# A hybrid decoder step on one core: sample attention taken four batches at a time, with zero-padded queries and probabilities

## The chip, the cores and the metric

The kernel runs on one core of one Trainium2 chip. The metric is the device time of one launch in microseconds (us). Three unprofiled runs of the kernel before took 1790.85, 1792.77 and 1795.26 us, so its median is 1792.77 us. One profiled execution, whose rows are quoted below, took 1795.69 us.

## The reference

One layer of a decoder with two parallel groups of heads is computed for 256 prompt tokens and for 8 sample batches of 8 new tokens each (320 token columns in all), model width 2048:

```python
p = rmsnorm(x) @ w_in                       # 3*1024 attention columns, 4*1024 delta-rule columns, 16 more
att = attend(q_att, k_att, v_att)           # 8 heads of 128
gdn = gated_delta_rule(...)                 # 8 heads of 128
x = x + concat(att, gdn) @ w_out
x = x + conv_ffn(rmsnorm(x))                # 2048 -> 2*5632 -> 2048
```

The part that is changed is `attend` for the sample tokens. Each of the 8 batches has 256 past keys and values in two pages of 128 rows of a paged cache, named by a page table, and its own 8 new tokens:

```python
lo = einsum('bqhd,bkhd->bqhk', q, k_own) * scale + rel_bias(own)    # causal inside the batch
ls = einsum('bqhd,bqhsd->bqhs', q, k_past) * scale + rel_bias(past)
p  = softmax(concat([ls, lo]))
out = p[..., :256] @ v_past + p[..., 256:] @ v_own
```

## The kernel before

**The stream of projections.** All weight products run on TensorE as a stream of chunks. A chunk is 512 rows by 256 columns of a weight: it is loaded by a queue of SyncE, split by ScalarE (`w_hi`, L687) and VectorE (`w_lo`, L1044) into a high and a low part, three chunks ahead of its use, and used in 24 matmuls with 320 moving columns (lines L1554 to L1556). There are 144 chunks before the feed-forward part (`g0`, `g1`, `a0`, `a1`, `wg`, `wa0`, `wa1`: the input projection by groups of heads, then the output projection) and 264 in it.

**Small steps between the quarters.** The delta rule and the attention are cut into steps such as `("P", "SS", g, b)`: the engine (P TensorE, A ScalarE, V VectorE, G GpSimd), the name, the half `g` of the heads (4 heads each) and a batch. `schedule()` places the chain of steps into the quarters of the chunks. A quarter is 6 projection matmuls and counts 10 units; a TensorE step adds 0.85 times its entry in `LENGTH` to the clock `at`; a step of another engine pushes back `ready`, the earliest place of the next TensorE step, by its `LENGTH` less 1 (GpSimd: less 4); no step is placed before the chunk that stands beside it in the chain. Each engine then works through its own list in this order, and waits by semaphores for the steps that it needs. Nothing of the schedule is known to the chip: where a step comes too early, TensorE waits and the projections wait behind it. GpSimd has nothing between its steps here, so it issues a load as soon as its semaphores allow.

**Attention steps of the half g** (`att_steps`): `hk` loads and flips the table of relative biases (hankel, 512 KB) and VectorE writes `bias_q` and `bias_s` from it; `kv` turns the new keys and values and stores them; `S`, `E`, `N`, `T`, `O` are the prompt's attention head by head. Then, for each batch b of the sample tokens:

- `pk`, `pv`: GpSimd reads two page numbers and issues two loads of 256 KB each, of keys and of values, two batches deep in `k_pages` and `v_pages`.
- `kt`: 8 transposes of key pages on TensorE; ScalarE and VectorE copy one half each to `k_t_past` (L861, L1347).
- `SS`: scores; for each head one matmul of 8 query columns against 256 past keys (L1907) and one against the 64 new keys (L1908), the four heads at the partitions 0, 32, 64 and 96 of the output.
- `SS`, `SE`, `SN` on VectorE, ScalarE, VectorE: scale, bias and maximum (L1352 to L1356); exponential and sum (L864); reciprocal and product (L1359, L1360).
- `PT`: three transposes of the probabilities, copied by ScalarE; `PV`: 8 matmuls on the pages (L1921) and 4 on the new values (L1924), each with 8 columns of probabilities stationary; `OT`: one transpose back.

The planner puts `SS` of one batch next to `OT` of the batch before it. In its slots, the first half's `hk` on TensorE stands in chunk 88 (quarter 3), `kv` in 92 (1), the first `kt` in 98 (0) and the last `OT` in 110 (3). The second half starts in chunk 113, its first `kt` stands in 119 (3) and its last `OT` in 132 (2). The output projection's last part begins at chunk 136 and needs them.

Of the kernel before, what the change touches and what calls it, by code (L numbers as in the profile page):

```python
# [17 lines left out]
F32 = mybir.dt.float32  # L18
# [6 lines left out]
P = 128  # L25
# [23 lines left out]
def constants():  # L49
# [15 lines left out]
    }  # L65
    cb, rb = np.arange(BLK)[None, :], r % BLK
# [178 lines left out]


def ffn_param_steps():
    s = []
    for r in range(5):
# [144 lines left out]
def build(nc, I, O):  # L394
# [80 lines left out]
    kst = a.put("k_tok", [P, 2, 4, P])  # L475
    hk = a.put("hankel", [P, 4, 2 * P])
    bm = a.put("bias_q", [P, 4, 2 * P])
    bs = a.put("bias_s", [P, 2 * P + 120])
    sc = a.put("scores", [P, 2, 384])
    pt = a.put("probs_t", [P, 2, 384])  # L480
    ktp = a.put("k_t_past", [P, 4, 2 * P])
    kp = a.put("k_pages", [P, 2, 2, 4, P])
    vp = a.put("v_pages", [P, 2, 2, 4, P])
# [45 lines left out]

    def over_free(ap, count):  # L530

        return ap.unsqueeze(2).broadcast_to([ap.shape[0], ap.shape[1], count])
# [18 lines left out]
    def sem(name):  # L551
        sems[name] = nc.alloc_semaphore(name)
        return sems[name]
# [12 lines left out]
    pk_in, pv_in, s_in, s_out = ([sem(f"{k}{i}") for i in range(2)] for k in ("k_pages_in", "v_pages_in", "state_in", "state_out"))  # L566
# [53 lines left out]
    with block:  # L620
# [57 lines left out]
        def _(act):  # L678
# [51 lines left out]
            def step(x):  # L730
# [131 lines left out]
                elif name == "SE":  # L862
                    after(act, "V", "SS", *k)
                    finish(act.activation(sc[:, 0, 0:TOK], sc[:, 0, 0:TOK], ACT.Exp, bias=ast[:, 0, 0:1], accum_out=ast[:, 0, 2:3]))  # L864
                elif name == "PT":
                    after(act, "P", "PT", *k)
                    act.activation(pt[:, 0, 0:256], b3[:, 0:256], ACT.Copy)
                    finish(act.activation(pt[0:NS, 0, 256:384], b3[0:NS, 256:384], ACT.Copy))
                elif name == "PV":
                    after(act, "P", "PV", *k)  # L870
                    finish(act.activation(ob[:, :], b0[:, 0:P], ACT.Copy))
                elif name == "OT":
                    g, b = k
                    after(act, "P", "OT", *k)
                    finish(act.activation(reg[g][:, 0:4, SEQ + b * DT:SEQ + b * DT + DT],
                                          b1[:, 0:P].rearrange("p (h s) -> p h s", h=4)[:, :, 0:DT], ACT.Copy))
# [6 lines left out]
                elif name == "ma":  # L883
                    g = k[0]
                    act.wait_ge(mm_done, FIRST["wg"])
                    after(act, "A", "OT", g, DB - 1)
# [144 lines left out]
        def _(dve):  # L1031
# [59 lines left out]
            def step(x):  # L1091
# [218 lines left out]
                elif name == "hk":  # L1310
                    g = k[0]
                    after(dve, "P", "hk", g)
                    chain(dve.tensor_copy(bm[:, :, :], psB[:, 2:4, :].rearrange("p k (h x) -> p (k h) x", h=2)))
                    if g == 0:
                        dve.memset(bs[:, 0:2 * P], 0.0)
                        dve.memset(bs[:, 2 * P:], NEG)
                    chain(tt(bm[:, :, P:2 * P], bm[:, :, P:2 * P], over_heads(C("causal"), 4), ALU.add))
                    for h in range(4):
                        row = bs[32 * h:32 * h + DT]
                        dve.tensor_copy(row[:, 0:P], bm[0:DT, h, 0:1].broadcast_to([DT, P]))  # L1320
                        dve.tensor_copy(row[:, P:2 * P], bm[0:DT, h, 0:P])
                        ins = dve.tensor_copy(row[:, 2 * P + 56:2 * P + 64], bm[0:DT, h, P:P + DT])
                    finish(ins)
# [21 lines left out]
                elif name == "kt":  # L1345
                    after(dve, "P", "kt", *k)
                    finish(dve.tensor_copy(ktp[:, :, P:2 * P], heads(b1, P)))  # L1347
                elif name == "SS":
                    g, b = k
                    after(dve, "P", "SS", g, b)  # L1350
                    o_ = 2 * P + 56 - DT * b
                    dve.scalar_tensor_tensor(out=sc[:, 0, 0:256], in0=b2[:, 0:256], scalar=SCALE, in1=bs[:, 0:256],  # L1352
                                             op0=ALU.mult, op1=ALU.add)
                    chain(dve.scalar_tensor_tensor(out=sc[:, 0, 256:TOK], in0=b2[:, 256:TOK], scalar=SCALE,
                                                   in1=bs[:, o_:o_ + NS], op0=ALU.mult, op1=ALU.add))
                    finish(dve.tensor_reduce(ast[:, 0, 0:1], sc[:, 0, 0:TOK], AX.X, ALU.max, negate=True))  # L1356
                elif name == "SN":
                    after(dve, "A", "SE", *k)
                    chain(dve.reciprocal(ast[:, 0, 4:5], ast[:, 0, 2:3]))  # L1359
                    finish(dve.tensor_scalar(sc[:, 0, 0:TOK], sc[:, 0, 0:TOK], ast[:, 0, 4:5], None, ALU.mult))  # L1360
# [181 lines left out]
        def _(pe):  # L1542
# [54 lines left out]
            def step(x):  # L1597
# [251 lines left out]
                elif name == "hk":  # L1849
                    g = k[0]  # L1850
                    pe.wait_ge(hk_in, 16 * (g + 1))
                    after(pe, *(("V", "us", 1, 3) if g == 0 else ("A", "OT", 0, DB - 1)))
# [4 lines left out]
                elif name == "kv":  # L1857
# [3 lines left out]
                    after(pe, *(("A", "kv", g, t - 1) if t else ("V", "hk", g)))  # L1861
# [21 lines left out]
                elif name == "O":  # L1883
# [5 lines left out]
                    finish(pe.matmul(b3[:, P:SEQ], vt[:, 1, h, :], pt[:, h % 2, SEQ:SEQ + P], start=False, stop=True))  # L1889
                elif name == "kt":  # L1890
                    g, b = k
                    pe.wait_ge(pk_in[b % 2], 32 * (DB // 2 * g + b // 2 + 1))
                    after(pe, *(("A", "O", g, 3) if b == 0 else ("V", "SS", g, b - 1)))
                    if b >= 2:
                        after(pe, "A", "OT", g, b - 2)
# [4 lines left out]
                elif name == "SS":  # L1900
                    g, b = k
                    after(pe, "A", "kt", g, b)
                    after(pe, "V", "kt", g, b)
                    c0 = SEQ + b * DT
# [381 lines left out]
```

## Time and profile before

| | |
|---|---|
| median of three runs | 1792.77 us (1790.85 to 1795.26) |
| the profiled execution | 1795.69 us, of which the span from first to last instruction is 1794.0 us |
| TensorE busy | 1700.9 us, 95% of the span |
| VectorE, ScalarE, GpSimd busy | 1070.7, 665.4, 206.0 us |
| mean granted TensorE clock | 0.989 |
| bytes moved by DMA | 258.29 MB, 144 GB/s in the mean |

Busy time says how long an engine had work in it, not how fast it got on; the place where this kernel's time is set is read from the starts of the projection matmuls, which follow each other evenly wherever nothing comes between them.

### The profile page before, as it was taken

Reading aid. Unit: us, or ns where it says so; the run is one execution under the profiler, and the core shown is the slowest. Engines: PE = TensorE matmul, PEld = TensorE weight load, DVE = VectorE, ACT = ScalarE, POOL = GpSimd, SP = SyncE. Lnnn points to the kernel's source line nnn. Section 1 sums busy time; section 2 is a strip of 40 time slices with the busy share of each in tenths; the row PEclk is TensorE's granted clock in tenths of the full one; section 3 lists DMA queues with packets and bytes.
Section 4 is the critical chain, followed back from the end, with each engine's and each line's share of the span. In section 5 each row is a group of like instructions: output and inputs, shape, how many; then the busy total and the mean of one; then the engine's idle time right before and its main releaser. Section 6 shows DMA issues by size and latency. Waiting matters only on the chain.

```text
span 1794.0 us, 31685 instructions
## 1 busy us (share of the span) xinstructions
PE 1700.9 (95%) x13245; PEld 1618.7 (90%) x13245; DVE 1070.7 (60%) x1744; ACT 665.4 (37%) x932; POOL 206.0 (11%) x343
## 2 busy tenths in 40 slices
PE   4999998899988988999999999999999999999996
PEld 3998987898778778789999999999999999999995
DVE  5456676665534444456676666666667565666662
ACT  4453432443224444445333333333333333333332
POOL 1112123112121110100010000000000000000010
PEclk9999999999999999999999999999999999999999
DMA  6333345433574553533444444444444444444432
GB/s 184 108 117 108 106 124 155 128 106 113 165 235 134 185 186 123 189 121 122 147 150 155 149 146 152 142 157 149 153 153 147 148 153 153 144 150 153 152 128 68
DMA packets 229998, 258.29 MB, mean 144 GB/s; under 512 B 9052, under 2 KB 220574, under 8 KB 229216
## 3 DMA queue, kind: packets, MB, share of 16 engines
q1 hardware_dynamic: 216448, 220.14, 38.5%
q0 software_dynamic: 10720, 34.86, 6.4%
q8 instruction: 105, 1.72, 0.4%
q10 hardware_dynamic: 2688, 1.27, 0.3%
q14 instruction: 37, 0.30, 0.1%
HBM read 245.11 MB, written 11.12 MB: 143 GB/s over the span
## 4 chain that ended last, share of the span: by engine, by line
PE 79%; DVE 10%; issue 4%; DMA 3%; ACT 3%; POOL 1%; DVEq 0%; SPq 0%; POOLq 0%; ACTq 0%
PE ps_proj L1554 18%; PE ps_proj L1556 18%; PE ps_proj L1555 18%; PE ps_small L1554 5%; PE ps_small L1556 5%; PE ps_small L1555 5%; DVE w_lo L1044 3%; PE ps_small L1589 2%; ACT w_hi L687 2%; DMA state_s<-in_state_gdn_dram 1%; DMA x_raw<-in_x_sample_dram 1%; DVE conv_acc L1065 1%; DVE state_s L1039 1%; DMA out_ss_dram<-state_s 1%; PE ps_small L1921 0%
## 5 line engine op out<-in xcount | busy, mean ns | idle before, releaser
L1554 PE MATMUL ps_proj<-x_hi,w_hi 128*128 128x320 f32 x2560 | 822.7, 321 | 8.8 <-DVE x_lo L1039 4.6
L1556 PE MATMUL ps_proj<-x_hi,w_lo 128*128 128x320 f32 x2560 | 795.3, 311 | 0.0
L1555 PE MATMUL ps_proj<-x_lo,w_hi 128*128 128x320 f32 x2560 | 795.2, 311 | 0.0
L1044 DVE TENSOR_TENSOR w_lo<-w_raw,w_hi 128x1024 fp32r<-128x1024 f32 x408 | 506.2, 1242 | 456.1 <-ACT w_hi L687 455.0
L687 ACT ACTIVATE w_hi<-w_raw 128x1024 fp32r<-128x1024 f32 x408 | 431.3, 1058 | 719.5 <-PE ps_proj L1556 524.2
L1554 PEld LDWEIGHTS ps_proj<-x_hi,w_hi 128*128 128x128 f32 x2560 | 485.2, 190 | 30.5 <-issue 18.5
L1555 PEld LDWEIGHTS ps_proj<-x_lo,w_hi 128*128 128x128 f32 x2560 | 485.7, 190 | 2.4 <-issue 1.7
L1556 PEld LDWEIGHTS ps_proj<-x_hi,w_lo 128*128 128x128 f32 x2560 | 484.7, 189 | 0.0
L1554 PE MATMUL ps_small<-hid_hi,w_hi 128*128 128x320 f32 x704 | 218.2, 310 | 0.0
L1556 PE MATMUL ps_small<-hid_hi,w_lo 128*128 128x320 f32 x704 | 217.5, 309 | 0.0
L1555 PE MATMUL ps_small<-hid_lo,w_hi 128*128 128x320 f32 x704 | 217.5, 309 | 0.0
L2229 POOL TENSOR_TENSOR ffn_ext<-ffn_params_t,consts 128x16 f32<-128x16 f32 x88 | 52.4, 617 | 839.2 <-DVE ffn_acc L1437 814.8
L1554 PEld LDWEIGHTS ps_small<-hid_hi,w_hi 128*128 128x128 f32 x704 | 132.2, 188 | 1.6 <-DVE x_res L1039 1.6
L1555 PEld LDWEIGHTS ps_small<-hid_lo,w_hi 128*128 128x128 f32 x704 | 132.2, 188 | 0.0
L1556 PEld LDWEIGHTS ps_small<-hid_hi,w_lo 128*128 128x128 f32 x704 | 132.2, 188 | 0.0
L1039 DVE TENSOR_TENSOR x_res<-ps_small,x_res 128x640 f32<-128x640 f32 x88 | 72.4, 823 | 60.6 <-PE ps_small L1556 60.6
L1437 DVE SCALAR_TENSOR_TENSOR ffn_acc<-ffn_ext,ffn_params_t,ffn_acc 128x336 f32<-128x336 f32 x176 | 94.3, 567 | 3.9
L1039 DVE TENSOR_TENSOR ffn_ext<-ps_proj,root 128x512 f32<-128x512 f32 x132 | 41.7, 373 | 0.0
L1065 DVE SCALAR_TENSOR_TENSOR conv_acc<-u_ext,params_t,conv_acc 128x344 f32<-128x344 f32 x72 | 38.2, 572 | 0.6
L1435 DVE TENSOR_SCALAR ffn_acc<-ffn_ext,ffn_params_t 128x336 f32<-128x336 f32 x88 | 36.9, 451 | 0.0
L2073 POOL TENSOR_TENSOR small<-small 128x4 f32<-128x4 f32 (+5 forms) x17 | 22.0, 1297 | 105.3 <-DVE small L1279 31.4
L958 ACT ACTIVATE ffn_acc<-ffn_acc 128x672 f32<-128x672 f32 x22 | 16.9, 769 | 38.8 <-DVE ffn_acc L1437 38.8
(326 smaller groups left out, 1190.5 us busy)
## 6 DMA issues: line engine op xcount, KB each, us to landing
w_raw<-in_w_up_dram SPq DMA_DIRECT2D x176, 512.0 KB, 3.5
w_raw<-in_w_in_dram SPq DMA_DIRECT2D x112, 512.0 KB, 3.5
w_raw<-in_w_down_dram SPq DMA_DIRECT2D x88, 512.0 KB, 3.3
w_raw<-in_w_out_dram SPq DMA_DIRECT2D x32, 512.0 KB, 3.3
state_s<-in_state_gdn_dram POOLq DMA_DIRECT2D x16, 512.0 KB, 5.6
k_pages<-in_cache_k_dram POOLq DMA_DIRECT2D x32, 256.0 KB, 3.6
v_pages<-in_cache_v_dram POOLq DMA_DIRECT2D x32, 256.0 KB, 3.4
out_ss_dram<-state_s POOLq DMA_DIRECT2D x8, 512.0 KB, 4.5
```

The costliest lines, as they stand in the source:

```text
L687: act.activation(whi[:, slot], raw[:, slot], ACT.Copy).then_inc(hi_done, 1)
L1039: return dve.tensor_tensor(out, a_, b_, op)
L1044: dve.tensor_tensor(wlo[:, slot], raw[:, slot], whi[:, slot].bitcast(F32), ALU.subtract).then_inc(lo_done, 1)
L1065: ins = dve.scalar_tensor_tensor(out=acc[:, j, 0:344], in0=u, scalar=wcol, in1=acc[:, j, 0:344], op0=ALU.mult, op1=ALU.add)
L1435: ins = dve.tensor_scalar(facc[:, kind, j, 0:336], u, w_(2), w_(3), ALU.mult, ALU.add)
L1437: ins = dve.scalar_tensor_tensor(out=facc[:, kind, j, 0:336], in0=u, scalar=w_(tap), in1=facc[:, kind, j, 0:336], op0=ALU.mult, op1=ALU.add)
L1554: pe.matmul(o, hi, rhs_hi[:, k0 + kk_, :], start=first and kk_ == 0, stop=False)
L1555: pe.matmul(o, hi, rhs_lo[:, k0 + kk_, :], start=False, stop=False)
L1556: ins = pe.matmul(o, lo, rhs_hi[:, k0 + kk_, :], start=False, stop=last and kk_ == CQ - 1)
L1589: return pe.transpose(out, in_, C("ident", n, n))
L2073: return pool.tensor_tensor(out, in_, sm("mh", n, 0, width), ALU.pow)
L2229: ins = pool.tensor_tensor(fue[:, kind, j, 2 + SEQ:338].rearrange("p (b s) -> p b s", b=DB)[:, :, 0:2], old, C("ones", P, 16).rearrange("p ...
```

## The change

For the sample tokens, four batches share one softmax. The 32 queries of four batches and one head fill 32 partitions. `q_z` holds them as four blocks that are zero but for the 8 queries of one batch, so the scores of four batches add up in one PSUM tile: `SS` still runs per batch, with 32 stationary columns, and the product with the new keys runs once per four. The steps `SS`, `SE`, `SN` of VectorE and ScalarE, and `PT`, `PV`, `OT`, run twice per half instead of eight times. ScalarE copies the transposed probabilities into zeroed blocks (`probs_z`), so that `PV` adds up four batches. GpSimd clears both (`qz`), VectorE fills the queries. `bias_s` is made by a new pair of steps `hb`: four matmuls that repeat the first 8 rows over 32 partitions, and five VectorE instructions in place of twelve small copies. `v_pages` grows to four batches, the biases' table shares its space with the fourth, so the second table is loaded after the first half's last `PV` instead of right behind the first `hk`. `k_pages` stays at two. In the order, `kt` of the next batch follows `SS` at once, and `PT`, `PV`, `OT` of the first four batches are spread over the batches 4 to 6. `LENGTH` gets new values.

```diff
+    parts["rep8"] = r == np.arange(32)[None, :] % DT
+    parts["own"] = own
+    parts["ownneg"] = np.where(own, 0.0, NEG)
...
 def att_steps(g):
-    s = ([] if g else [("G", "hk", g)]) + [("G", "pk", g, 0), ("G", "pv", g, 0), ("G", "pk", g, 1), ("G", "pv", g, 1), ("P", "hk", g), ("V", "hk", g)]
-    if g == 0:
-        s += [("G", "hk", 1)]
+    s = [("G", "hk", g), ("G", "pk", g, 0)] + [("G", "pv", g, b) for b in range(3)] + [("G", "pk", g, 1), ("P", "hk", g), ("V", "hk", g)]
+    s += [("G", "pv", g, 3), ("P", "hb", g), ("V", "hb", g)]
...
-    s += [("P", "kt", g, 0), ("A", "kt", g, 0), ("V", "kt", g, 0), ("G", "pk", g, 2)]
-    for b in range(DB):
-        s += [("P", "SS", g, b), ("V", "SS", g, b), ("A", "SE", g, b)]
-        if b < DB - 1:
-            s += [("P", "kt", g, b + 1), ("A", "kt", g, b + 1), ("V", "kt", g, b + 1)]
-            if b < DB - 3:
-                s += [("G", "pk", g, b + 3)]
-        s += [("V", "SN", g, b), ("P", "PT", g, b), ("A", "PT", g, b), ("P", "PV", g, b),
-              ("A", "PV", g, b), ("P", "OT", g, b), ("A", "OT", g, b)]
-        if b < DB - 2:
-            s += [("G", "pv", g, b + 2)]
+    s += [("P", "kt", g, 0), ("G", "qz", g), ("A", "kt", g, 0), ("V", "kt", g, 0), ("V", "qz", g, 0)]
+    soft = []
+    for q in range(2):
+        for b in range(4 * q, 4 * q + 4):
+            s += [("P", "SS", g, b)]
+            if b < DB - 2:
+                s += [("G", "pk", g, b + 2)]
+            s += soft[:1]
+            if b < DB - 1:
+                s += [("P", "kt", g, b + 1)] + soft[1:3] + [("A", "kt", g, b + 1), ("V", "kt", g, b + 1)]
+            soft = soft[3:]
+            if b == 3:
+                s += [("V", "SS", g, 0), ("V", "qz", g, 1), ("A", "SE", g, 0), ("V", "SN", g, 0)]
+                soft = [("P", "PT", g, 0), ("A", "PT", g, 0), None,
+                        ("P", "PV", g, 0), ("A", "PV", g, 0), None,
+                        ("P", "OT", g, 0), ("A", "OT", g, 0), None]
+            s = [x for x in s if x]
+            if ("P", "PV", g, 0) in s and ("G", "pv", g, 4) not in s:
+                s += [("G", "pv", g, 4 + j) for j in range(4)]
+    s += [("V", "SS", g, 1), ("A", "SE", g, 1), ("V", "SN", g, 1), ("P", "PT", g, 1), ("A", "PT", g, 1), ("P", "PV", g, 1),
+          ("A", "PV", g, 1), ("P", "OT", g, 1), ("A", "OT", g, 1)]
...
-          "ks": 13, "us": 22, "sh": 11, "hk": 20, "kv": 12, "S": 11, "O": 12, "kt": 17, "SS": 11, "PV": 11, "OT": 2, "ab": 76},
-    "A": {"sc2": 25, "sc5": 20, "ab": 10, "qs": 12, "cp": 0, "tb1": 10, "o": 12, "kv": 12, "E": 11, "SE": 7, "fp": 22},
+          "ks": 13, "us": 22, "sh": 11, "hk": 20, "kv": 12, "S": 11, "O": 12, "kt": 10, "hb": 6, "SS": 6, "PT": 4, "PV": 16, "OT": 2, "ab": 76},
+    "A": {"sc2": 25, "sc5": 20, "ab": 10, "qs": 12, "cp": 0, "tb1": 10, "o": 12, "kv": 12, "E": 11, "SE": 9, "kt": 8, "PT": 9, "fp": 22},
...
-          "S": 13, "SS": 17, "SN": 7},
-    "G": {"rn": 29, "or": 14, "so": 0, "si": 0, "s2": 0, "gs": 0, "kv": 0, "pk": 0, "pv": 0, "hk": 100, "mk": 6, "xd": 0},
+          "S": 13, "SS": 15, "SN": 7, "kt": 8, "hb": 12, "qz": 3},
+    "G": {"rn": 29, "or": 14, "so": 0, "si": 0, "s2": 0, "gs": 0, "kv": 0, "pk": 0, "pv": 0, "hk": 100, "mk": 6, "xd": 0, "qz": 0},
...
+                    for h in range(4):
+                        ins = pe.matmul(b2[32 * h:32 * h + 32, 0:P + DT], C("rep8"), bm[:, h, 0:P + DT], start=True, stop=True)
...
-                    for h in range(4):
-                        qT = reg[g][:, h, c0:c0 + DT]
-                        pe.matmul(b2[32 * h:32 * h + DT, 0:256], qT, ktp[:, h, :], start=True, stop=True)
-                        ins = pe.matmul(b2[32 * h:32 * h + DT, 256:TOK], qT, reg[g][:, 4 + h, SEQ:TOK], start=True, stop=True)
+                    if j == 0:
+                        after(pe, "V", "qz", g, q)
+                        if q:
+                            after(pe, "V", "SS", g, 0)
+                        for h in range(4):
+                            pe.matmul(b2[32 * h:32 * h + 32, 256:TOK], reg[g][:, h, SEQ + 32 * q:SEQ + 32 * q + 32],
+                                      reg[g][:, 4 + h, SEQ:TOK], start=True, stop=True)
+                    for h in range(4):
+                        ins = pe.matmul(b2[32 * h:32 * h + 32, 0:256], qz[:, P * j + 32 * h:P * j + 32 * h + 32], ktp[:, h, :],
+                                        start=j == 0, stop=j == 3, skip_group_check=True)
...
+                    for j in range(4):
+                        pe.wait_ge(pv_in[j], 32 * (2 * g + q + 1))
+                        for i in range(2):
+                            for h in range(4):
+                                at = P * j + 32 * h
+                                pe.matmul(b3[32 * h:32 * h + 32, 384:512], pz[:, i, at:at + 32], vp[:, j, i, h, :],
+                                          start=j == 0 and i == 0, stop=False, skip_group_check=True)
...
-                        after(pool, "P", "hk", 0)
+                        after(pool, "P", "PV", 0, 1)
...
+                elif name == "qz":
+                    g = k[0]
+                    after(pool, "A", "O", g, 3)
+                    for i in range(2):
+                        pool.wait_ge(kv_out[i], 32 * ((2, 1), (3, 3))[g][i])
+                    pool.memset(qz[:, :], 0.0)
+                    finish(pool.memset(pz[:, :, :], 0.0))
```

`probs_z` is 2 by 544 columns and `q_z` 544; ScalarE's `PT` copies become two of 128 by 128 into the blocks of `probs_z` and one of 64 by 128.

## Rows read from the trace of the kernel before

**Rows 1.** The page: busy time, share of the span and instructions of each engine

```profile
PE 1700.9 (95%) x13245; PEld 1618.7 (90%) x13245; DVE 1070.7 (60%) x1744; ACT 665.4 (37%) x932; POOL 206.0 (11%) x343
```

**Rows 2.** TensorE's waits, 520 to 860 us: total, times, longest

```profile
PE ps_small L1589 <- DVE scores L1360: 8.8, 12, 1.4
...
PE ps_small L1589 <- DVE bias_s L1322: 1.5, 1, 1.5
...
PE ps_small L1907 <- DVE k_t_past L1347: 0.7, 1, 0.7
```

**Rows 3.** Timeline of TensorE around one batch: start, us, instruction, idle time before

```profile
575.68 0.39 PE L1554 MATMUL ps_proj<-x_hi,w_hi 128*128 128x320 f32 x1
...
577.74 0.55 PE L1589 MATMUL ps_small<-consts,scores 128*128 128x128 f32 x3 [0.94 <-DVE scores L1360]
578.04 0.39 PE L1554 MATMUL ps_proj<-x_hi,w_hi 128*128 128x320 f32 x1
...
579.09 0.62 PE L1921 MATMUL ps_small<-v_pages,probs_t 128*8 128x128 f32 x16
579.64 0.40 PE L1924 MATMUL ps_small<-v_tok,probs_t 64*8 64x128 f32 x8
579.98 0.42 PE L1554 MATMUL ps_proj<-x_hi,w_hi 128*128 128x320 f32 x1
...
581.16 0.64 PE L1907 MATMUL ps_small<-k_t_past,reg 128*8 128x256 f32 x8
581.59 0.32 PE L1908 MATMUL ps_small<-reg 128*8 128x64 f32 x8
581.84 0.41 PE L1554 MATMUL ps_proj<-x_hi,w_hi 128*128 128x320 f32 x1
582.09 0.31 PE L1555 MATMUL ps_proj<-x_lo,w_hi 128*128 128x320 f32 x1
...
584.28 0.31 PE L1555 MATMUL ps_proj<-x_lo,w_hi 128*128 128x320 f32 x1
...
585.37 0.39 PE L1554 MATMUL ps_proj<-x_hi,w_hi 128*128 128x320 f32 x1
```

**Rows 4.** Timeline of TensorE: a step of the delta rule with 32 stationary columns

```profile
468.44 1.08 PE L1827 MATMUL ps_small<-state_s,reg 128*32 128x128 f32 x32 [0.40 <-DMA state_s<-in_state_gdn_dram]
```

**Rows 5.** Groups of VectorE and of ScalarE, 569 to 650 us, shapes apart

```profile
L1044 DVE TENSOR_TENSOR w_lo<-w_raw,w_hi 128x1024 fp32r<-128x1024 f32 x14 | 17.2, 1225 | 26.9 <-ACT w_hi L687 26.9
...
L861 ACT ACTIVATE k_t_past<-ps_small 128x512 f32<-128x512 f32 x8 | 4.8, 599 | 4.9 <-PE ps_small L1589 4.9
```

**Rows 6.** Timeline of GpSimd: the two key pages of batch 3 as they are issued

```profile
577.13 0.67 POOL L2182 DMA_DIRECT2D k_pages<-in_cache_k_dram  x1 [4.02 <-issue]
578.27 0.55 POOL L2182 DMA_DIRECT2D k_pages<-in_cache_k_dram  x1 [0.47 <-issue]
```

**Rows 7.** The page: DMA issues, KB each, us from issue to landing

```profile
state_s<-in_state_gdn_dram POOLq DMA_DIRECT2D x16, 512.0 KB, 5.6
k_pages<-in_cache_k_dram POOLq DMA_DIRECT2D x32, 256.0 KB, 3.6
v_pages<-in_cache_v_dram POOLq DMA_DIRECT2D x32, 256.0 KB, 3.4
```

**Rows 8.** Timeline of TensorE: the first bias table

```profile
517.69 3.78 PE L1854 MATMUL ps_small<-hankel,consts 128*128 128x512 f32 x4 [7.11 <-DMA hankel<-rb_scratch]
```

**Rows 9.** Groups of GpSimd: clearing 1024 columns

```profile
L2111 POOL MEMSET reg<- 128x1024 f32 x2 | 1.9, 975 | 0.0
```

**Rows 10.** Stretches: PE, PEld, DVE, ACT, POOL busy, clock, DMA share, GB/s

```profile
516.00:522.00 6.00, 4.31 (x7) 2.24 (x8) 0.49 (x1) 0.00 (x0) 2.58 (x5) 0.50 0.74 251
652.00:658.60 6.60, 5.99 (x22) 6.02 (x23) 3.05 (x3) 1.68 (x3) 0.00 (x0) 0.50 0.26 86
696.30:699.60 3.30, 3.30 (x15) 3.30 (x14) 0.22 (x1) 2.42 (x6) 0.00 (x0) 0.50 0.00 0
569.00:650.00 81.00, 75.59 (x746) 64.99 (x744) 34.24 (x62) 33.31 (x74) 17.58 (x32) 1.00 0.58 189
```

More of the change, by code:

```diff
@@ L474, in build @@
     vt = a.put("v_tok", [P, 3, 4, P])
[L475 to L478, printed above, removed]
+    kst_at = a.at
+    pz = a.put("probs_z", [P, 2, 4 * (P + DT)])
+    kst = nc.alloc_sbuf_tensor_at("k_tok", [P, 2, 4, P], F32, offset=kst_at)
+    po = a.put("probs_own", [P, P])
+    ktp_at = a.at
+    ktp = a.put("k_t_past", [P, 4, 2 * P])
+    bm = nc.alloc_sbuf_tensor_at("bias_q", [P, 4, 2 * P], F32, offset=ktp_at)
+    bs = a.put("bias_s", [P, 2 * P + 96])
     sc = a.put("scores", [P, 2, 384])
+    pt_at = a.at
     pt = a.put("probs_t", [P, 2, 384])
-    ktp = a.put("k_t_past", [P, 4, 2 * P])
+    qz = nc.alloc_sbuf_tensor_at("q_z", [P, 4 * (P + DT)], F32, offset=pt_at)
     kp = a.put("k_pages", [P, 2, 2, 4, P])
-    vp = a.put("v_pages", [P, 2, 2, 4, P])
+    vp_at = a.at
+    vp = a.put("v_pages", [P, 4, 2, 4, P])
+    hk = nc.alloc_sbuf_tensor_at("hankel", [P, 4, 2 * P], F32, offset=vp_at + 3 * 4096)
     ob = a.put("o_tok", [P, P])
@@ L1313, in step @@
                     chain(dve.tensor_copy(bm[:, :, :], psB[:, 2:4, :].rearrange("p k (h x) -> p (k h) x", h=2)))
+                    finish(tt(bm[:, :, P:2 * P], bm[:, :, P:2 * P], over_heads(C("causal"), 4), ALU.add))
+                elif name == "hb":
+                    g = k[0]
+                    after(dve, "P", "hb", g)
                     if g == 0:
-                        dve.memset(bs[:, 0:2 * P], 0.0)
-                        dve.memset(bs[:, 2 * P:], NEG)
-                    chain(tt(bm[:, :, P:2 * P], bm[:, :, P:2 * P], over_heads(C("causal"), 4), ALU.add))
-                    for h in range(4):
[L1319 to L1323, printed above, removed]
+                        dve.memset(bs[:, 2 * P:2 * P + 32], NEG)
+                        dve.memset(bs[:, 2 * P + 64:], NEG)
+                    dve.tensor_copy(bs[:, 0:P], b2[:, 0:1].broadcast_to([P, P]))
+                    dve.tensor_copy(bs[:, P:2 * P], b2[:, 0:P])
+                    win = bs[:, 2 * P + 32:2 * P + 64].rearrange("p (j s) -> p j s", j=4)
+                    chain(tt(win, over_heads(b2[:, P:P + DT], 4), over_free(C("own"), DT), ALU.mult))
+                    finish(tt(win, win, over_free(C("ownneg"), DT), ALU.add))
                 elif name == "S":
@@ L1889, in step @@
                     finish(pe.matmul(b3[:, P:SEQ], vt[:, 1, h, :], pt[:, h % 2, SEQ:SEQ + P], start=False, stop=True))
+                elif name == "hb":
+                    g = k[0]
+                    after(pe, "V", "hk", g)
+                    for h in range(4):
+                        ins = pe.matmul(b2[32 * h:32 * h + 32, 0:P + DT], C("rep8"), bm[:, h, 0:P + DT], start=True, stop=True)
+                    finish(ins)
                 elif name == "kt":
@@ L1909, in step @@
                     finish(ins)
                 elif name == "PT":
+                    q = k[1]
                     after(pe, "V", "SN", *k)
-                    turn(b3[:, 0:P], sc[:, 0, 0:P], P)
-                    turn(b3[:, P:2 * P], sc[:, 0, P:2 * P], P)
-                    finish(turn(b3[0:NS, 2 * P:3 * P], sc[:, 0, 2 * P:TOK], P))
+                    after(pe, *(("A", "OT", k[0], 0) if q else ("A", "O", k[0], 3)))
+                    turn(b3[:, 0:P], sc[:, q, 0:P], P)
+                    turn(b3[:, P:2 * P], sc[:, q, P:2 * P], P)
@@ L1915, in step @@
+                    finish(turn(b3[0:NS, 2 * P:3 * P], sc[:, q, 2 * P:TOK], P))
                 elif name == "PV":
-                    g, b = k
-                    pe.wait_ge(pv_in[b % 2], 32 * (DB // 2 * g + b // 2 + 1))
-                    after(pe, "A", "PT", g, b)
-                    for i in range(2):
-                        for h in range(4):
-                            pe.matmul(b0[32 * h:32 * h + DT, 0:P], pt[:, 0, i * P + 32 * h:i * P + 32 * h + DT],
-                                      vp[:, b % 2, i, h, :], start=i == 0, stop=False)
+                    g, q = k
@@ L1923, in step @@
                     for h in range(4):
[L1924 to L1925 removed]
+                        ins = pe.matmul(b3[32 * h:32 * h + 32, 384:512], po[0:NS, 32 * h:32 * h + 32], vt[0:NS, 2, h, :],
+                                        start=False, stop=True, skip_group_check=True)
                     finish(ins)
@@ L1928, in step @@
                     after(pe, "A", "PV", *k)
-                    finish(turn(b1[:, 0:P], ob[:, :], P))
+                    finish(turn(b3[:, 0:P], ob[:, :], P))
                 elif name == "fp":
@@ L2172, in step @@
                     g, b = k
+                    if name == "pk":
+                        slot = b % 2
+                        if b > 1 or g:
+                            after(pool, "P", "kt", *((g, b - 2) if b > 1 else (0, DB - 2 + b)))
+                        cache, tile_, arrived = I["cache_k"], kp, pk_in
+                    else:
+                        slot = b % 4
+                        if b > 3 or g:
+                            after(pool, "P", "PV", *((g, 0) if b > 3 else (0, 1)))
+                        if b == 3:
+                            after(pool, "P", "hk", g)
+                        cache, tile_, arrived = I["cache_v"], vp, pv_in
                     if (g, b) == (0, 0):
```

75 lines of the change are left out of this document (45 added, 30 removed).

## The prediction

> **What bounds the kernel.** I read the page first: TensorE has work for 1700.9 of 1794.0 us, VectorE for 60% [rows 1]. So time is worth having only on TensorE's queue, in two kinds: work taken out of it, and waits taken out of it. Next the list of TensorE's waits over the attention [rows 2]: no wait on weights is in it, but 12 waits on the sample tokens' softmax, 8.8 us, and single ones of 0.7 and 1.5 us. Last the timeline of one batch [rows 3], the main source. The projections start every 2.19 / 15 = 0.146 us (582.09 to 584.28). Whatever stretches an interval between two projections beyond 0.146 us for each, a small step has put into the queue.
>
> **Price of a batch before** [rows 3], each interval less its projections:
> - `PT`, 575.68 to 578.04, 6 projections (0.88): 1.48 us. Of it 0.94 is the wait. Three transposes are three eighths of `kt`'s price, 0.34; the remaining 0.20 is the restart after a wait.
> - `PV`, to 579.98: 1.06.
> - `OT` and `SS`, to 581.84: 0.98; `OT` is one transpose, 0.11, so `SS` is 0.87.
> - `kt`, to 585.37, 18 projections: 0.90.
>
> Work without waits: 0.34 + 1.06 + 0.98 + 0.90 = 3.28 us, times 16 batches = 52.5 us. Waits: 8.8 + 12 x 0.2 = 11.2, and 0.7 and 1.5: 13.4 us [rows 2].
>
> **The same work after.** `kt` stays, 16 x 0.90 = 14.4. In `SS` the four heads' passes run side by side: from 581.16 to 581.59 two sets of 256 columns pass in 0.43, so 64 columns cost 0.054 a set. Two such sets leave twelve of the sixteen batches: `SS` is 0.76 x 16 = 12.2, and 0.4 for the four that remain. `PT` and `OT` run four times: 1.4 and 0.4. `PV` had 24 passes in 6 sets of four, and now has 18 sets. A set of 128 columns takes 0.11 us with 32 stationary columns (32 passes in 1.08, the last one's own 0.27 taken off [rows 4]) and (0.62 - 0.27) / 3 = 0.12 with 8 [rows 3]: padding to 32 columns is free. So `PV` is 1.06 + 12 x 0.11 = 2.38, times 4 = 9.5. The new `hb` is an `SS` with 136 in place of 256 columns, 0.56, twice: 1.1. Sum 39.4 us: **13.1 us less work**. The bounds: if `SS` and `kt`, now adjacent, save one restart, 16 x 0.1 less; if 32 columns paid twice for a set, 8 more for `PV`.
>
> The Trainium skill, "TensorE: Matmul & The Clock Gate", section "LDWEIGHTS (loading the stationary operand)", speaks against the padding: the load takes as long as its columns, at 1.2 GHz. Four loads of 32 columns would then need 107 ns a set and hold back only the sets of 64 columns; by that rule the sum would lose an estimated 0.4 us. The trace has no such set at 32 columns.
>
> **Where the steps go.** By the planner's arithmetic `hk` of the first half comes one quarter earlier, since one more GpSimd step of -4 units stands before it (88, quarter 2). `kv` no longer waits for the second table's 96 units: 90 (2), and the first `kt` 96 (1). In the batches a `kt` and the next `SS` are two quarters apart; the lap is 2 x 0.88 + 0.76 + 0.90 = 3.4 us, where before it was 585.37 - 575.68 = 9.7. The last `OT` stands in 102 (1). The second half begins in 113 as before, its `hk` 9 quarters later, its first `kt` in 122 (2), its end in 128 (2), eight chunks before `wa1`. So no deadline is touched, but **the cover of every wait shrinks to a third**. The waits after:
>
> - *Key pages.* GpSimd may load batch b+2 once `kt` of b is done. The second page of batch 3 is issued at 578.27 [rows 6] and takes 3.6 us [rows 7]: there at 581.9, 6.2 us after TensorE left `kt` at 575.68. The new order wants it after 3.4 + 1.75 + 0.76 = 5.9. So 0.3 us is missing twice in each half (batches 2 and 4; the odd ones gain what the even ones lost, and behind batch 4 five quarters of softmax follow). If landings take 5.6, the longest of GpSimd's page-sized loads [rows 7], 2.3 is missing. I take 1.0, nearer to the row of pages: 4 x 1.0 = 4.0.
> - *Copies of `kt` before `SS`.* Two quarters are 1.75 us. The copy takes 0.60 on ScalarE; VectorE may first finish a weight part of 1.23 [rows 5]: about 0.5 missing when it does, for about a third of 14: 14 x 0.15 = 2.1 (nothing to 7). `SS` of batch 6 stands one quarter behind its `kt`; that case costs 0.7 in the trace [rows 2] when the weight part is in the way: 2 x 0.5.
> - *Softmax.* The first four's has more than a batch of cover. The last four's has three quarters, 2.6 us. In the trace the lap from `SS` to its probabilities is longer than the 4 quarters and a `kt` it was given, by 0.94 [rows 3], weight part and `kt` copy included. I take 1.0 twice (nothing to 2.3: both weight parts).
> - *Value pages for the last four.* They are issued together, some 9 us for eight issues 1.14 apart [rows 6], and land 3.4 later, about 12.9 after the first `PV`. The second `PV` reaches its fourth batch after about as long; 0.5 for the load on the DMA engines, 0.3 for the third copy of `PT`, twice: 1.6 (nothing to 5).
> - *`hb` before `kv`:* 0.3 twice. *First bias table:* TensorE already waits 7.1 us for it [rows 8]; a quarter earlier means 0.9 more, since the load comes no sooner. The second table is loaded some ten chunks ahead and hides.
> - *Clearing on GpSimd:* 1632 columns at 0.975 us a thousand [rows 9] are 1.6 us behind the last `O`, and `SS` comes 2.6 behind: hidden, 0.4 to spare once VectorE has filled the queries. It would cost what exceeds that.
>
> Sum 4.0 + 3.1 + 2.0 + 1.6 + 0.6 + 0.9 = 12.2 against 13.4: 1.2 less. ScalarE and VectorE lose work, but they are not the bound. Together 13.1 + 1.2 = **14.3 us less**. The profiled 1795.7 would be 1781.4; it ran 2.9 us above the median, so the median becomes **1778.5 us**. A difference of 0.3% (5.4 us) is about what can be told from none.
>
> **The rivals.**
> - *Waits vanish more than I allow.* Three stretches ran at clock 0.50, that is 1.2 GHz, the first inside the 7.1 us wait [rows 8, 10]; 6.6 us held 22 matmuls that need 3.2 at 2.4 GHz [rows 10], so such a stretch costs 3.4, the short one at 696 us 1.6. It lies in prompt steps that now fall elsewhere in the chunk. With all bounds at their low ends (pages 1.2, table 0.9) the waits are 2.1, the total 24 us, with that stretch 26. About 1771, for a part of it. Chance 0.16.
> - *The short laps give back half.* Pages, copies and softmax at the middle of their upper ranges: 20 us of waits instead of 12.2: 1786. Chance 0.17.
> - *The weights stop hiding.* In the sample stretch DMA moved 189 GB/s at a share of 0.58 [rows 10]. Now 5 MB of pages and 3 MB of weights come in about 45 us, 180 GB/s; only the burst of value pages is above. If the stream lagged, the time would stay at 1793. The ring of three chunks speaks against it. Chance 0.04.
> - *Slower: the key pages become the bound.* One mechanism, a landing of L us in place of 3.6. Every 0.1 adds 0.4 us over the four waits. The 7.1 us wait went with a stretch at half clock; two such stretches would add 6.8. The gain is gone at 14.3 - 6.8 = 7.5 us more waiting, 1.9 each, thus beyond what I counted at L = 6.2; at 8 us the kernel takes 1800. For it: short laps, eight issues in a row. Against: 5.6 is the longest median in this queue, for double the bytes. Chance 0.05. The Trainium skill, "SBUF — State Buffer", section "SBUF: two separate sides", names a cause that would do it: GpSimd cannot write its loads' descriptors while VectorE runs a copy in a two-port mode. Here pages landed in 3.6 us with VectorE busy 34.2 of 81.0 us [rows 7, 10], and new copies read PSUM; the trace gives that rule no support yet.
>
> **How the numbers follow.** My forecast has 0.58, over 1772 to 1784 us. Faster by over 0.3% (below 1787.4): 0.58 + 0.16 + 0.10 of the half-gain case = 0.84; within: 0.07 + 0.04 = 0.11; slower: 0.05. From 1768 to 1788 lie my case, nearly all of the first rival and most of the second: 8 in 10.
>
> **What the changed profile would show.** The projections between the small steps still 0.146 us apart; `PV` 16 times 4 passes and 8 more in about 2.4 us, four times; `kt` plus `SS` about 1.7 us a lap; TensorE's waits on scores down from 8.8 to about 2; new waits of TensorE on key pages, 2 to 4 in all. The first sample stretch, 81 us, should be about 45 us long for its eight batches. Wrong would make me: waits on pages above 2 us each, a set of 32 columns slower than 0.11 us, further stretches at clock 0.50, or a wait on `q_z`.

## The result, and the profile after

| | before | changed |
|---|---|---|
| median of the runs timed together | 1793.80 us (1790.85 to 1795.26) | 1774.94 us (1770.60 to 1777.92) |
| ratio, 95% interval | | 0.9895, 0.987 to 0.992 |
| profiled execution | 1795.69 us | 1770.60 us |
| the attention, in the profiles (below) | 296.9 us | 272.9 us |

The kernel is 18.9 us faster, where 14.3 us (1778.5 us) was forecast. In two more timings, unaltered, the ratio was 0.9896 and 0.9904 (below). So the mechanism stands, and the gain was about a third larger than the sum made it.

TensorE's waits over the attention after the change (total, times, longest), which answer to [rows 2]:

```profile
PE ps_small L1892 <- DMA hankel<-rb_scratch: 8.3, 1, 8.3
PE ps_small L1627 <- DVE scores L1373: 4.5, 6, 2.1
PE ps_small L1977 <- DMA v_pages<-in_cache_v_dram: 4.3, 4, 2.3
...
PE ps_small L1627 <- DMA k_pages<-in_cache_k_dram: 0.5, 1, 0.5
PE ps_small L1627 <- DVE scores L1398: 0.5, 1, 0.5
```

The wait on the sample softmax has gone from 8.8 us to 0.5 (L1398 is the L1360 of before). A wait on value pages is new. The prompt's softmax (L1373) waits 4.5 us and the first bias table 8.3 us; neither is the change's subject.

The timeline of TensorE around the first and the second `PV` of the first half, now with 32 stationary columns:

```profile
585.94 0.31 PE L1594 MATMUL ps_proj<-x_hi,w_lo 128*128 128x320 f32 x1
586.18 0.64 PE L1959 MATMUL ps_small<-k_t_past,q_z 128*32 128x256 f32 x8
586.64 1.93 PE L1977 MATMUL ps_small<-v_pages,probs_z 128*32 128x128 f32 x64
588.50 0.42 PE L1980 MATMUL ps_small<-v_tok,probs_own 64*32 64x128 f32 x8
588.85 1.09 PE L1627 MATMUL ps_small<-consts,k_pages 128*128 128x128 f32 x8
589.70 0.39 PE L1592 MATMUL ps_proj<-x_hi,w_hi 128*128 128x320 f32 x1
...
599.59 1.08 PE L1977 MATMUL ps_small<-v_pages,probs_z 128*32 128x128 f32 x32
601.11 0.65 PE L1977 MATMUL ps_small<-v_pages,probs_z 128*32 128x128 f32 x16 [0.44 <-DMA v_pages<-in_cache_v_dram]
603.02 0.64 PE L1977 MATMUL ps_small<-v_pages,probs_z 128*32 128x128 f32 x16 [1.26 <-DMA v_pages<-in_cache_v_dram]
603.59 0.42 PE L1980 MATMUL ps_small<-v_tok,probs_own 64*32 64x128 f32 x8
603.94 0.41 PE L1592 MATMUL ps_proj<-x_hi,w_hi 128*128 128x320 f32 x1
```

The first `PV` passes 64 times in 1.93 us: (1.93 - 0.27) / 15 = 0.111 us a set of four, so padding to 32 columns costs nothing ([rows 4] gives 0.116 by the same sum). The second one stops twice. GpSimd issued the last of its eight value loads at 598.12, and the last batch's matmuls start at 603.02.

**Where the time went.** I compare the attention between two points that stand before and behind it in both traces: from the restart of the projections after the last transpose of `gdn_new` to the restart after the first one of `ffn_rows`. In the kernel before:

```profile
502.42 0.39 PE L1554 MATMUL ps_proj<-x_hi,w_hi 128*128 128x320 f32 x1
...
799.10 0.47 PE L1589 MATMUL ps_small<-consts,ffn_rows 88*128 88x88 f32 x4
799.35 0.39 PE L1554 MATMUL ps_proj<-x_hi,w_hi 128*128 128x320 f32 x1
```

and in the changed one:

```profile
501.28 0.39 PE L1592 MATMUL ps_proj<-x_hi,w_hi 128*128 128x320 f32 x1
...
773.97 0.47 PE L1627 MATMUL ps_small<-consts,ffn_rows 88*128 88x88 f32 x4
774.22 0.39 PE L1592 MATMUL ps_proj<-x_hi,w_hi 128*128 128x320 f32 x1
```

That is 296.9 and 272.9 us with the same 1212 projections, 176.6 us at 0.1457. The rest is summed interval by interval, like the prediction's price of a batch. An interval without a small step in it can be too long as well: the first one behind a small step always is, by 0.08 to 0.11 us (the restart), and every one in a stretch at half clock. This is counted with the step before it:

| us beside the projections | before | changed |
|---|---|---|
| sample steps `kt` to `OT`, with their waits | 65.8 | 46.3 |
| `hb` | | 1.1 |
| bias tables, with the wait for the first | 13.1 | 14.0 |
| turning the new keys (`kv`) | 9.3 | 8.0 |
| the prompt's attention | 24.4 | 21.9 |
| wait before the output projection, and the rest | 7.8 | 5.1 |
| sum | 120.3 | 96.4 |

How the slow restart behind the first table stands apart from `hb`, in the changed kernel:

```profile
519.67 1.25 PE L1592 MATMUL ps_proj<-x_hi,w_hi 128*128 128x320 f32 x1
520.73 0.35 PE L1593 MATMUL ps_proj<-x_lo,w_hi 128*128 128x320 f32 x1
...
525.99 0.44 PE L1932 MATMUL ps_small<-bias_q,consts 128*32 128x136 f32 x8
526.36 0.41 PE L1592 MATMUL ps_proj<-x_hi,w_hi 128*128 128x320 f32 x1
```

The change's own part is 65.8 - 46.3 - 1.1 = 18.4 us, and the `kv` behind the new `hb` gives 1.3. The other 4.3 us are 2.5 in the prompt's steps, 2.7 behind the output projection's wait, where before has a stretch at half clock and the changed profile has none, less 0.9 for the table. They come from the clock and from where prompt steps stand, and are not shown to belong to the change. With the second and third profile of the changed kernel the own part is 16.0 and 18.6 us. The first profiled execution was also the fastest of its four timed ones, and by the timed medians 17 to 19 us belong to the change.

### The profile page after: what moved, and what is told of

The parts are those of the page before. It is cut to its first block, busy times and chain, and to the rows that moved or that the text cites. A ratio compares the mean times of both kernels' runs of the same rounds, so it can differ in the third digit from the quotient of the medians.

```text
span 1768.9 us, 31108 instructions
## 1 busy us (share of the span) xinstructions
PE 1682.3 (95%) x13021; PEld 1607.7 (91%) x13021; DVE 1052.3 (59%) x1672; ACT 647.8 (37%) x864; POOL 210.0 (12%) x347
## 4 chain that ended last, share of the span: by engine, by line
PE 80%; DVE 7%; issue 4%; DMA 4%; ACT 2%; POOL 1%; POOLq 0%; DVEq 0%; SPq 0%; ACTq 0%
PE ps_proj L1592 19%; PE ps_proj L1593 18%; PE ps_proj L1594 18%; PE ps_small L1592 5%; PE ps_small L1594 5%; PE ps_small L1593 5%; PE ps_small L1627 2%; DVE w_lo L1071 2%; DMA state_s<-in_state_gdn_dram 1%; ACT w_hi L711 1%; DVE conv_acc L1092 1%; DMA x_raw<-in_x_sample_dram 1%; DVE state_s L1066 1%; DMA v_pages<-in_cache_v_dram 1%; DMA out_ss_dram<-state_s 1%
```

## The experiments

Each kernel is the changed one with the edit shown, but for the one that says otherwise. Kernels of one group ran on one chip beside the same runs of the kernel before. The groups are: second timing, bias table late, second `PV` late and no late value loads; `kt` twice, before spaced, key pages in quarters and all late; third timing and short laps. The second group has no unaltered changed kernel in it, so its members are compared with that kernel by their ratios. "Attention" is the time between the two points above in the profiled execution; it leaves out what the clock did in other phases. The kernel before has 296.9 us there. One profile each carries it, and the three of the changed kernel differ by 3 us (272.1 to 275.1).

| kernel | ratio to before, 95% | median us | attention us |
|---|---|---|---|
| changed, second timing | 0.9896 (0.9879 to 0.9914) | 1777.0 | 275.1 |
| changed, third timing | 0.9904 (0.9881 to 0.9928) | 1776.5 | 272.1 |
| bias table late | 0.9873 (0.9853 to 0.9892) | 1771.4 | 265.7 |
| second `PV` late | 0.9869 (0.9846 to 0.9891) | 1771.4 | 269.5 |
| no late value loads | 0.9847 (0.9830 to 0.9863) | 1766.7 | 265.5 |
| `kt` twice | 0.9945 (0.9930 to 0.9959) | 1783.1 | 282.7 |
| kernel before, spaced | 0.9964 (0.9952 to 0.9975) | 1787.7 | 286.7 |
| key pages in quarters | 1.0039 (1.0024 to 1.0055) | 1800.0 | 302.5 |
| short laps | 0.9962 (0.9941 to 0.9984) | 1786.1 | 285.4 |
| all late | 0.9787 (0.9772 to 0.9801) | 1753.5 | 254.0 |

**The changed kernel again, twice.**

> The changed kernel, unaltered, beside the kernel before. My account (work of the small steps, waits, half-clock stretches): 14 to 25 us faster than before; in the attention the same waits as in the first profile (bias table 8, value pages 4, key pages under 1 us), while the stretches at clock 0.50 fall elsewhere. Rival (the 24 us between the two profiles is all gain): 24 us again with the same stretches.

> The changed kernel again, unaltered, beside the run with short laps: 1.0 to 1.2% faster than before, as in its first two runs; waits as there. Stretches at clock 0.50 elsewhere again.

The medians are 19.4 and 17.2 us below before's. The waits are the same (value pages 5.5 and 4.1 us, key pages 0.6 and 0.5). The expectation of 14 to 25 us held, and the rival, 24 us by the times, did not; the attention alone is 21.8 and 24.8 us shorter. The third ratio, 0.9904, is just short of the 1.0% that I had set as its lower end.

**How much was only a matter of place?** The kernel before, no work changed:

```diff
-          "S": 13, "SS": 17, "SN": 7},
+          "S": 13, "SS": 17, "SN": 17},
```

> The kernel before with LENGTH of VectorE's SN 17 in place of 7, so each PT stands one quarter (0.88 us) later; no work is changed. If the 8.8 us of waits on the softmax and their restarts were a matter of place alone: 7 to 10 us faster than the kernel before, and about half of the change's gain to be had without it. Rival (the wait moves to the next step): within 2 us of the kernel before.

The softmax waits fell from 8.8 to 2.0 us. The kernel is 6.2 us faster by the medians, below the 7 to 10 that I expected. The attention is 10.2 us shorter, but 2.8 of that is the stretch at half clock behind the output projection's wait, which this profile does not have; the sample steps give 7.1 (65.8 to 58.7).

```profile
PE ps_small L1589 <- DVE scores L1360: 2.0, 4, 0.8
```

Four waits, 2.0 us, stayed. So waits of this kind are a loss of about one for one, the rival that they move on is out, and about a third of the change's gain, not the half that I expected, was to be had by the order alone.

**Is TensorE's queue still the bound, and what do longer laps do?**

```diff
-                    for i, bank in ((0, b0), (1, b1)):
+                    for i, bank in ((0, b0), (1, b1), (0, b0), (1, b1)):
                         for h in range(4):
                             ins = turn(bank[:, h * P:(h + 1) * P], kp[:, b % 2, i, h, :], P)
```

> Each kt transposes its eight key blocks twice, 128 transposes more. If TensorE's queue sets the time one for one, they cost 16 x 0.80 = 12.8 us over the unaltered changed kernel (0.10 us each, less the restart that is paid already). Rival (the laps are bound by the copies of ScalarE and VectorE or by the key pages, which hide TensorE's work): under 8 us.

By the ratios, 0.9945 against 0.9896 and 0.9904, the kernel is 7 to 9 us slower, below the 12.8 that I expected and at the rival's edge. The intervals show where the rest is. Each `kt` costs 0.87 us more, 13.9 in all. But the second `PV` of the two halves, 10.7 us in the changed kernel, takes 6.6:

```profile
PE ps_small L1977 <- DMA v_pages<-in_cache_v_dram: 1.3, 1, 1.3
```

Longer laps give the value pages their cover back, and 4 us return. So TensorE's queue is the bound, and the wait on values is a matter of time between the first `PV` and the second.

**The wait on value pages, from two sides.** The second `PV` later:

```diff
-    "A": {..., "SE": 9, "kt": 8, "PT": 9, "fp": 22},
+    "A": {..., "SE": 9, "kt": 8, "PT": 39, "fp": 22},
```

> LENGTH of ScalarE's PT 39 in place of 9, so the second PV of each half stands three quarters (2.6 us) further behind its PT. If the wait on value pages (4.3 us in all, with 1.7 us of a half-clock stretch and restarts) is only a matter of place: 4 to 7 us faster than the unaltered changed kernel, no wait on value pages. Rival (DMA engines or GpSimd are behind for good): the wait stays over 2 us.

and the loads left out, with `pv_in` waiting on the first four alone. The second `PV` then multiplies the pages of the batches 0 to 3 again, so this kernel leaves out the sample outputs of the last four batches:

```diff
-                s += [("G", "pv", g, 4 + j) for j in range(4)]
+                s += []
...
-                        pe.wait_ge(pv_in[j], 32 * (2 * g + q + 1))
+                        pe.wait_ge(pv_in[j], 32 * (g + 1))
```

> The values of batches 4 to 7 are not loaded; the second PV of each half multiplies the pages of batches 0 to 3 again, so the sample outputs of the last four batches are left out. If only waiting for these loads is lost: no wait on value pages, 4 to 7 us faster than the unaltered changed kernel, like the late second PV. If their 4 MB in two bursts also slow the weights: more than that, over 8 us.

In both the wait is gone. Placing `PV` later makes the kernel 5.6 us faster by the medians, as expected, though its ratio, 0.9869, overlaps the unaltered one's. The attention is 5.6, 2.7 and 3.4 us shorter than in the second, third and first profile of the changed kernel. The sample steps alone, 41.5 us against 46.1 to 48.7, show it more clearly. Leaving the loads out brings 9.6 us against the second profile, 10.3 by the medians. That is over the 8 us that I had set for slowed weights, but neither trace has a wait on weights. Between the two kernels lie 4 us, and the first has 3.4 us more of small waits:

```profile
PE ps_small L1912 <- ACT v_tok L867: 2.0, 2, 1.6
PE ps_small L1627 <- DMA k_pages<-in_cache_k_dram: 1.9, 4, 0.8
...
PE ps_small L1627 <- DVE scores L1398: 1.2, 1, 1.2
```

against 1.2, 0.5 and none without the loads. The reason for these I have not separated.

**The rival on the slower side: key pages as the bound.** Four transfers of 32 rows for each page, the same bytes:

```diff
+                        for r_ in (range(0, P, 32) if name == "pk" else (0,)):
+                            n_ = 32 if name == "pk" else P
+                            pool.dma_start(tile_[r_:r_ + n_, slot, i].rearrange("p h d -> p (h d)"),
+                                           src.rearrange("a s c -> (a s) c")[r_:r_ + n_]).then_inc(arrived[slot], 16)
...
-                    pe.wait_ge(pk_in[b % 2], 32 * (DB // 2 * g + b // 2 + 1))
+                    pe.wait_ge(pk_in[b % 2], 128 * (DB // 2 * g + b // 2 + 1))
```

> Each key page of the changed kernel is loaded in four transfers of 32 rows in place of one: same bytes, four times the issues. The rival 'key pages become the bound': GpSimd needs 2 x (0.6 + 4 x 0.54) = 5.5 us a batch against a lap of 3.4, so TensorE waits for keys 7 to 10 us in each half, and the kernel is 14 to 22 us slower than the unaltered changed one, about as slow as before. If the pages have more cover than I gave them: under 7 us slower.

```profile
PE ps_small L1627 <- DMA k_pages<-in_cache_k_dram: 18.7, 6, 3.8
PE ps_small L1892 <- DMA hankel<-rb_scratch: 8.0, 1, 8.0
PE ps_small L1912 <- ACT v_tok L867: 5.6, 2, 5.2
```

The waits on keys, 9.2 and 9.5 us in the halves, are in the expected range. The kernel is 1800.0 us, slower than the kernel before and by the ratios 24 to 26 us slower than the changed one, where I expected 14 to 22: eight stretches at half clock in the attention, where the changed kernel's first profile has three, and a wait of 5.2 us on the turned keys come on top. So late keys cost at least what the rival said. How near the real kernel is to that, the next run tells.

**By how little: short laps.**

```diff
-    "A": {..., "SE": 9, "kt": 8, "PT": 9, "fp": 22},
+    "A": {..., "SE": 9, "kt": 3, "PT": 9, "fp": 22},
...
-          "S": 13, "SS": 15, "SN": 7, "kt": 8, "hb": 12, "qz": 3},
+          "S": 13, "SS": 15, "SN": 7, "kt": 3, "hb": 12, "qz": 3},
```

> The changed kernel with LENGTH of the kt copies 3 in place of 8 on ScalarE and VectorE: one quarter in place of two between kt and SS, no work changed. Laps shrink from 3.3 to 2.5 us. If pages need some 6.3 us from the end of kt(b) until kt(b+2) may start: about 2 us of waiting on keys every second batch, 8 to 12 us in all, and longer waits on values; 8 to 15 us slower than the unaltered changed kernel. Rival (lap length does not matter, as copies and pages had room to spare): within 3 us.

```profile
PE ps_small L1627 <- DMA k_pages<-in_cache_k_dram: 5.8, 4, 1.9
PE ps_small L1977 <- DMA v_pages<-in_cache_v_dram: 5.4, 5, 2.8
...
PE ps_small L1959 <- DVE k_t_past L1376: 1.8, 2, 0.9
```

One quarter less a lap, and 9.6 us of the gain are gone (1786.1 against 1776.5 beside it), with the attention 13.2 us longer. The loss is in the range of 8 to 15, but not by the keys alone: their waits are 1.5 us each and 5.8 in all, where I had said 2 and 8 to 12. The copies of `kt` now make TensorE wait too, 0.9 us twice (L1376).

**The bias table, and all waits together.**

```diff
-    "G": {..., "hk": 100, "mk": 6, "xd": 0, "qz": 0},
+    "G": {..., "hk": 200, "mk": 6, "xd": 0, "qz": 0},
```

> LENGTH of GpSimd's hk 200 in place of 100, so TensorE reaches the bias table ten quarters later. If the wait for the first table (8.3 us) and the half-clock stretch around it are pure loss: the wait is gone, 9 to 10 us faster than the unaltered changed kernel. Rival (what follows is late as well, the wait comes back at kv or at the value pages): 0 to 3 us faster.

```profile
PE ps_small L1892 <- DMA hankel<-rb_scratch: 0.2, 1, 0.2
```

The wait is gone, and the tables' steps fell from 12.7 to 14.0 us in the three profiles of the changed kernel to 4.0, the 9 to 10 us that I expected. The kernel did not gain as much. The medians differ by 5.7 us, the intervals of the ratios overlap, and the attention is 9.4, 7.2 and 6.4 us shorter than in the second, first and third profile. So the result lies between my two cases: some 2.6 us came back in the prompt's steps, where waits on its softmax went from 4.5 to 6.1 and those on the turned keys from 0.8 to 1.8.

```diff
-    "A": {..., "kv": 12, "E": 11, "SE": 9, "kt": 8, "PT": 9, "fp": 22},
+    "A": {..., "kv": 22, "E": 11, "SE": 9, "kt": 8, "PT": 39, "fp": 22},
...
-          "S": 13, "SS": 15, "SN": 7, "kt": 8, "hb": 12, "qz": 3},
+          "S": 13, "N": 15, "SS": 15, "SN": 7, "kt": 8, "hb": 12, "qz": 3},
...
-    "G": {..., "hk": 100, "mk": 6, "xd": 0, "qz": 0},
+    "G": {..., "hk": 200, "mk": 6, "xd": 0, "qz": 0},
```

> The changed kernel with four longer entries: GpSimd hk 200, ScalarE PT 39 and kv 22, VectorE N 15 (5 before). Waits on the first table, value pages, turned keys and prompt softmax (8.3 + 4.3 + 2.3 + 4.5 us in the profile) should all but vanish, with half-clock stretches at 510, 678 and 739 us: 20 to 27 us faster than the unaltered changed kernel. Rival (the later end of the second half, chunk 134, brings a new wait before the output projection): under 15 us.

```profile
PE ps_proj L1592 <- issue: 4.1, 2, 3.0
PE ps_small L1627 <- DMA k_pages<-in_cache_k_dram: 3.7, 4, 1.5
PE ps_proj L1592 <- DVE x_res L1066: 1.9, 1, 1.9
PE ps_small L1627 <- DVE scores L1373: 0.9, 2, 0.5
```

1753.5 us: 40 us faster than before by the medians, and 20 to 23 faster than the changed kernel (20 to 21 by the ratios, 23 by the medians), with the same work. The second half's last step now stands in chunk 134, and the wait of 1.9 us on `x_res` is all that the late end could have brought. The key pages wait 3.7 us here, 3.0 of it at two of the second half. Those two landed 4.8 us after their issue, at 702.86 and 711.13, where in the changed kernel most pages took 3.0 to 3.8; why they took longer stays open.

## Why the prediction was right, and where its sum was not

- **The work.** Right. With the late value loads left out, the sample steps cost 39.0 us, 0.5 of it a wait, so 38.5 are work; the terms `kt`, `SS`, `PT`, `OT`, `PV` of the forecast sum to 38.3, and `hb` cost the 1.1 that it was given. The second `PV` without a wait (second `PV` late) takes 2.4 us, as forecast. The product with the new keys in 32 stationary columns adds 0.11 us to `SS` and `kt` (1.62 against 1.51 us), two sets at 0.054: the loss of an estimated 0.4 us, which the prediction named as a possibility for these sets, did not come. The first sample stretch is 42.9 us long, 45 were said.
- **The places.** Right to the quarter: the matmuls of the two tables, the first `kt`, the last `OT`. The first table's wait grew from 7.1 to 8.3 us, where 0.9 more was said; in the later profiles it was 7.8 and 6.6.
- **Copies of `kt` before `SS`: 3.1 us forecast, none measured.** This term is the one that failed by its reasoning. I let VectorE be caught in a weight part about every third time. In the first profile of the changed kernel it is caught in none of the sixteen copies: fifteen times it stands idle when the transposes are done, and once it is 0.56 us late behind an addition to `x_res`, which two quarters cover. The timeline shows one of them:

```profile
566.99 0.60 ACT L885 ACTIVATE k_t_past<-ps_small 128x512 f32<-128x512 f32 x1 [2.87 <-PE ps_small L1627]
566.99 0.69 DVE L1376 COPY k_t_past<-ps_small 128x512 f32<-128x512 f32 x1 [2.64 <-PE ps_small L1627]
...
567.48 1.05 ACT L711 ACTIVATE w_hi<-w_raw 128x1024 fp32r<-128x1024 f32 x1
...
568.57 1.23 DVE L1071 TENSOR_TENSOR w_lo<-w_raw,w_hi 128x1024 fp32r<-128x1024 f32 x1 [0.89 <-ACT w_hi L711]
568.64 0.64 PE L1959 MATMUL ps_small<-k_t_past,q_z 128*32 128x256 f32 x8
```

  ScalarE takes its `kt` copy first and the weight's high part after it, and VectorE's low part can only follow the high part. So here the weight part falls behind the copy, and `SS` starts while it runs. In seven others the last thing before the copy is a weight part, and it has ended 0.21 to 3.07 us before. That this holds every time is a matter of where the chunks' parts stand, and in one case by little.
- **Key pages: 4.0 forecast, 0.5 measured.** The gap of 0.3 us from the row was the better value; I had taken 1.0 for a fuller DMA. The second page of batch 3 was issued at 569.29, 2.6 us behind the restart at 566.71, just as [rows 6] has it, and it landed 3.2 us later, where [rows 7] has 3.6.
- **Softmax of the last four: 2.0 forecast, 0.5 measured.** The row of before included a weight part and a `kt` copy. Here no copy lies between, but a weight part still does: it holds up the first of the softmax's instructions.

```profile
594.65 1.23 DVE L1071 TENSOR_TENSOR w_lo<-w_raw,w_hi 128x1024 fp32r<-128x1024 f32 x1 [1.33 <-ACT w_hi L711]
595.80 0.42 DVE L1389 SCALAR_TENSOR_TENSOR scores<-ps_small,bias_s 128x256 f32<-128x256 f32 x1
```

- **Value pages: 1.6 forecast, 4.3 measured** (5.5 and 4.1 in the later profiles), with a stretch at half clock behind the longest wait. This is the term that was sized too small, for two reasons. I had set it against laps that contained the three waits above. Since those hardly came, the second `PV` started 10.7 us after the first had ended, where the 12.9 us of the prediction leave 11.5. And the last page landed 4.9 us after its issue, where I had 3.4, and 0.5 for the load on the DMA engines. The two runs from either side, and `kt` twice, show that the wait goes when `PV` comes later or the loads do not come at all.
- **`kv` and the prompt: 0.9 forecast (1.5 less 0.6), 3.8 in the one pair of profiles.** The wait on `bias_s` is gone as said, and `kv` gives 1.3 us. The 2.5 in the prompt's steps depend on the placing and on the clock.
- **Restarts.** The sum gave each wait before 0.2 us for the restart behind it, and none to the waits after. So it set unlike things against each other and flattered the change, by 2 to 3 us if the terms stand for a dozen waits.

Waits over the sample steps were so 5.3 us in place of 10.7; with their restarts and the half clock behind the longest they were about 7.8 (46.3 less the 38.5 of work). The sum had 14.3 us for the sample steps and `hb` (13.1 of work, and waits of 11.9 less 10.7), and the first pair of profiles shows 18.4: most of the 4 to 5 us by which the kernel is faster than forecast. That the total came out in the stated range is in part luck: on keys, copies and softmax 8.1 us of waits did not come, and against them stand 2.7 us more on the value pages and 2.5 us of restarts and half clock that the sum did not have. On the first three the low ends of the first rival came true and not the middle that the sum took; the value pages kept the total from that rival's 24 us. What the clock does in single executions, 7 us between the slowest and the fastest of four, is as large as this rest.

## What to carry to other kernels

Where a stream of large matmuls is the bound and small steps stand between them, price each small step by the intervals of the stream; then batching pays by the passes it removes, and a wait pays about one for one. When steps are packed closer, every load and copy loses cover at once, and a wait that is avoided in one place moves the need for the next load forward: count the cover of the last load with the laps free of waits. Before work is rebuilt, try the planner's lengths: four of them gave as much here as the whole change.

## What the runs showed of the chip

A wait does not always bring the half clock. The same wait of 3.0 us stands before the output projection in every profile. In the kernel before, 6.6 us at clock 0.50 follow it [rows 10]; in the changed kernel the clock stays full, as the stretch behind it shows (columns as in [rows 10]), while others are at half:

```profile
510.50:520.70 10.20, 3.82 (x5) 1.76 (x6) 0.00 (x1) 0.00 (x0) 4.58 (x8) 0.50 0.80 248
...
739.30:742.50 3.20, 3.20 (x30) 2.40 (x27) 0.00 (x0) 0.28 (x1) 0.00 (x0) 0.50 0.06 17
641.70:646.00 4.30, 4.30 (x30) 4.30 (x31) 2.37 (x2) 1.52 (x3) 0.00 (x0) 1.00 0.18 53
```

In the second profile of the same kernel the wait ends at 648.71, and 3.2 us at half clock begin some 1.6 us after it. The same profile has 13.5 us at half clock in the delta rule, where the first has two stretches of 3.4 us (281.8 and 302.3):

```profile
281.70:295.20 13.50, 13.06 (x82) 10.98 (x83) 4.15 (x8) 1.67 (x3) 3.52 (x6) 0.50 0.43 118
...
650.30:653.50 3.20, 3.20 (x14) 3.20 (x14) 0.84 (x1) 0.00 (x0) 0.00 (x0) 0.50 0.36 111
```

So the same program gets its half clock in other places each time. Since the program is the same, the two profiles can be set beside each other matmul by matmul, which shows where their 8.7 us arise. Counting the projection matmuls from 0, number 1200 starts at 283.94 and 284.00 us, number 1400 at 328.80 and 335.24, number 1500 at 358.76 and 363.64, number 3200 at 751.78 and 760.43. Behind that the difference stays at 8.65 us to the end. The 6.4 us up to number 1400 fall in with the long stretch at half clock and with a wait on `decay` that is 3.7 us long in place of 1.0. So the whole difference arises in the delta rule and the attention, and none of it in the feed-forward part. That is a reason to compare a stretch of the trace and not the whole time where a few us matter.
